# Part of a layer kernel rearranged: the state-space stage, its hand-over to the merge, one more expert block in the fixed schedule, and the latent stage

## The chip, the cores and the metric

The kernel runs on one core of a Trainium2 chip. The metric is the device time of one execution in microseconds, and the median of several runs is compared. Every time below is from one execution of the kernel before that was recorded with the hardware profiler, unless it says otherwise. TensorE is PE (its weight load PEld), VectorE DVE, ScalarE ACT, GpSimd POOL and SyncE SP.

## The reference, cut to what matters

Two transformer-like blocks run over 512 tokens of 1024 channels, in fp32. The parts that the change touches:

- State-space mixer: a projection gives x, B, C (24 tiles of 128 channels), a gate z (16 tiles) and a step width per head; a causal convolution of 4 taps and SiLU follow; then, in chunks, scores, states and outputs of 32 heads in 4 groups; at the end `y * silu(z)`, divided in each group by its root mean square (`rsqrt(mean(y*y) + 1e-6)`).
- Merge: `merged = g0 * y_att + g1 * y_pool + g2 * y_ssm`, with `g = sigmoid(h @ w_gate)`. The third gate is a product of h with 1024 columns, and `y_ssm` a product of the mixer's 2048 channels with `w_ssm_o`.
- Experts: each token goes to 2 of 16 experts, `(silu(x @ w1) * (x @ w3)) @ w2`, 512 wide.
- Latent projection of the second block: h @ w (448 columns), two root-mean-square norms of 256 and 128 channels, and a rotary embedding whose angles come from the positions.

## The kernel before

The program is a row of stages. In each, every engine has its own list of instructions and the lists are tied by semaphores; between two stages all engines meet. Matrix products at full precision are made of three: each fp32 operand is split into a high part (ACT writes it, rounded to the reduced fp32 type) and a low part (a subtraction on DVE), and PE multiplies high by high, high by low and low by high. So a weight tile has a chain: DMA, high part on ACT, low part on DVE, product on PE.

**State-space stage** (`ssm_stage`, from L1188). It forms 41 weight tiles of 1024x128, in the order of `ssm_tiles`: one for the step widths, 6 convolution tiles of group 0, and then for each group i the first four convolution tiles of group i+1, the four gate tiles of group i and the last two convolution tiles of group i+1. Tile t lies in `parts[t % 2]`, so its high part (`high`, L1415) waits for the product of tile t-2. `low` (L1543) is DVE's. The product is L1293, 24 matmuls of 128x512. PE's list for a group (from L1388) is: a tile, `turn_b` (L1307), a tile, `turn_x` 0 and 1 (L1315), a tile, `turn_x` 2 and 3, `chunk_products` (L1325), a tile, three `state`, `rows` and four times {a tile, `rows`, `heads`}, a tile, `squares`, a tile, `squares`. In the last group only the four gate tiles are left, and so the places before them are empty. `turn_x` waits until all six convolution tiles of its group have been convolved (L1558, L1560), bent (ACT's Tanh, L1443) and multiplied (L1576). `turn_b` waits for `std_done` of the group before, as both use bank 2. ACT's `root` (L1487) is a Sqrt, DVE's `invert` (L1686) a reciprocal, and then come four `normalise` passes (L1694). SP first stores x to DRAM and loads four small vectors (L1257 to L1263), and only then the next weight tiles; ACT waits for all four (L1493) before its other work on tile 0.

**Merge** (`merge_stage`, L1822). It works in halves, which are weight tiles of 1024x256 (`Halves`, L548: four slots of raw data, two of parts; `products` is L588, 48 matmuls each). For the third gate there are 12: 4 of the gate, 8 of `w_ssm_o` in two phases. DVE's `low(phase)` (L1914) makes the low parts of the mixer's output when a phase begins. Beside this DVE forms 8 strips of another product (`LaterStrips`, L1757): each is 2 MB from DRAM through a ring of two halves and 8 passes of DVE (`matvec`, L1787 and L1789). They are put behind the half-tiles of `STRIP_AT = (0, 1, 2, 4, 5, 6, 8, 9)`, and PE sums the first four (`ada.sums`) ahead of half-tile 6.

**Experts** (`experts_stage`, L2369). There is one block of 128 rows for each of the 16 experts, in a fixed, overlapped schedule. Rows beyond an expert's 128 go to further blocks, made in a loop of 7 with a condition (L2409, L2463, L2541, L2601): load, products in plain fp32 (L2469, L2482), nothing overlapped from one block to the next. In the recorded execution this loop's body ran once. The combine stage then gathers the rows (L2629).

**Latent** (`latent_stage`, L2675). SP loads the positions and the weights in the stage itself (L2697, L2698). PE's list is the angle product, four projections and two mean squares; ACT then takes a Sqrt of each, and DVE a reciprocal (L2750) and the scaling (L2753). The stage before it is `norm_stage` (L479).

## Time and profile before

| | |
|---|---|
| Median of 3 runs | 2955.51 us (2948.24 to 2959.59) |
| The profiled execution, its own time | 2950.82 us |
| Its span, first to last instruction | 2949.1 us |
| Mean granted TensorE clock | 0.922 of full speed |
| PE busy | 2589.5 us (88% of the span) |
| DVE busy | 1732.4 us (59%) |
| ACT busy | 1110.3 us (38%) |
| POOL busy | 47.6 us (2%) |

Busy time is an engine's sum over the whole span. What a part of the change can be worth is read from the stage it lies in: from the pieces of PE's time in which PE stood still there, and from what ended each of them. The state-space stage lies between 558 and 945 us, the merge from there to 1097 us, the experts' end and the combine stage around 1500 to 1600 us, and the latent stage between 1621 and 1676 us.

### The profile page before, as it was taken

Reading aid. Unit: us, or ns where it says so; the run is one execution under the profiler, and the core shown is the slowest. Engines: PE = TensorE matmul, PEld = TensorE weight load, DVE = VectorE, ACT = ScalarE, POOL = GpSimd, SP = SyncE. Lnnn points to the kernel's source line nnn. Section 1 sums busy time; section 2 is a strip of 40 time slices with the busy share of each in tenths; the row PEclk is TensorE's granted clock in tenths of the full one; section 3 lists DMA queues with packets and bytes.
Section 4 is the critical chain, followed back from the end, with each engine's and each line's share of the span. In section 5 each row is a group of like instructions: output and inputs, shape, how many; then the busy total and the mean of one; then the engine's idle time right before and its main releaser. Section 6 shows DMA issues by size and latency. Waiting matters only on the chain. (4 is left out here: it accounts for less than half of the span.)

```text
span 2949.1 us, 32640 instructions
## 1 busy us (share of the span) xinstructions
PE 2589.5 (88%) x12891; PEld 2014.7 (68%) x12891; DVE 1732.4 (59%) x2355; ACT 1110.3 (38%) x1586; POOL 47.6 (2%) x145
## 2 busy tenths in 40 slices
PE   7999799789987998499985698899997667799998
PEld 6777588567765875288862256788886666688886
DVE  6877625277776664599954364633447963643334
ACT  4333322135543222478842133532324123342333
POOL 0000000000000000100001000000000000000000
PEclk8999699899997999799997799999998788899999
DMA  7666537122212832499971121233231203223230
GB/s 252 222 213 205 196 96 271 44 72 64 65 51 71 287 128 87 163 392 417 414 281 64 53 66 57 72 100 88 98 100 17 31 2 114 86 86 100 87 100 29
DMA packets 285059, 393.61 MB, mean 133 GB/s; under 512 B 21400, under 2 KB 209291, under 8 KB 276204
## 3 DMA queue, kind: packets, MB, share of 16 engines
q1 hardware_dynamic: 277068, 361.65, 36.2%
q0 software_dynamic: 5392, 20.97, 1.8%
q10 hardware_dynamic: 2448, 8.91, 0.7%
q8 instruction: 102, 1.67, 0.2%
q14 instruction: 49, 0.40, 0.0%
HBM read 361.10 MB, written 30.41 MB: 133 GB/s over the span
## 5 line engine op out<-in xcount | busy, mean ns | idle before, releaser
L3248 PE MATMUL banks<-big,tail_w_parts 128*128 128x512 f32 x1920 | 444.0, 393 | 16.6 <-DVE tail_w_parts L3405 16.6
L3248 PEld LDWEIGHTS banks<-big,tail_w_parts 128*128 128x128 f32 x1920 | 363.9, 190 | 95.1 <-DVE tail_w_parts L3405 17.2
L3248 PE MATMUL banks<-h_parts_second,tail_w_parts 128*128 128x512 f32 x1440 | 332.9, 392 | 12.8 <-DVE h_parts_second L3430 12.8
L3405 DVE TENSOR_TENSOR tail_w_parts<-w_second,tail_w_parts 128x2048 fp32r<-128x2048 f32 x70 | 160.3, 2292 | 284.2 <-ACT tail_w_parts L3309 284.2
L3248 PEld LDWEIGHTS banks<-h_parts_second,tail_w_parts 128*128 128x128 f32 x1440 | 272.1, 189 | 71.0 <-issue 14.4
L1293 PE MATMUL banks<-h_parts,ssm_w_parts 128*128 128x512 f32 x984 | 244.0, 406 | 23.4 <-DVE ssm_xbc L1598 15.9
L1293 PEld LDWEIGHTS banks<-h_parts,ssm_w_parts 128*128 128x128 f32 x984 | 189.1, 195 | 71.7 <-DVE ssm_w_parts L1546 25.0
L2191 DVE TENSOR_TENSOR expert_parts<-w,expert_parts 128x2048 fp32r<-128x2048 f32 x96 | 219.4, 2289 | 30.7 <-ACT expert_parts L2187 30.3
L3309 ACT ACTIVATE tail_w_parts<-w_second 128x2048 fp32r<-128x2048 f32 x70 | 133.8, 1914 | 266.4 <-PE banks L3248 266.4
L2187 ACT ACTIVATE expert_parts<-w 128x2048 fp32r<-128x2048 f32 x96 | 183.4, 1916 | 60.2 <-PE banks L2198 60.2
L2198 PE MATMUL banks<-expert_parts,expert_xt 128*128 128x512 f32 x768 | 182.1, 397 | 5.1 <-DVE expert_xt L2563 5.1
L2198 PEld LDWEIGHTS banks<-expert_parts,expert_xt 128*128 128x128 f32 x768 | 145.6, 191 | 35.7 <-DVE expert_xt L2563 5.7
L597 PE MATMUL banks<-h_parts,ssm_parts 128*128 128x512 f32 x576 | 135.7, 398 | 14.7 <-DVE ssm_parts L586 11.5
L890 PE MATMUL banks<-h_parts,qkv_parts 128*128 128x512 f32 x552 | 145.5, 416 | 3.4 <-SPq L155 3.4
L597 PE MATMUL banks<-h_parts,front_parts 128*128 128x512 f32 x576 | 134.4, 395 | 8.5 <-DVE front_parts L586 6.4
L597 PEld LDWEIGHTS banks<-h_parts,ssm_parts 128*128 128x128 f32 x576 | 110.7, 193 | 39.8 <-DVE ssm_parts L586 12.5
L3439 DVE TENSOR_TENSOR tail_q<-tail_r 128x512 f32<-128x512 f32 x64 | 41.4, 688 | 159.7 <-ACT tail_r L3332 159.7
L597 PEld LDWEIGHTS banks<-h_parts,front_parts 128*128 128x128 f32 x576 | 109.6, 191 | 32.7 <-DVE front_parts L586 6.5
L890 PEld LDWEIGHTS banks<-h_parts,qkv_parts 128*128 128x128 f32 x552 | 106.1, 199 | 36.8 <-issue 11.4
L1095 DVE SCALAR_TENSOR_TENSOR attention_mod_sum<-w,silu_c,attention_mod_sum 128x512 f32<-128x512 f32 x168 | 126.1, 751 | 5.1
L3332 ACT ACTIVATE tail_r<-banks,cols 128x512 f32<-128x512 f32 x64 | 40.5, 685 | 204.9 <-PE banks L3248 204.9
L2198 PE MATMUL banks<-expert_parts,expert_ht 128*128 128x512 f32 x384 | 94.1, 402 | 4.5 <-DVE expert_ht L2568 4.5
(628 smaller groups left out, 3821.0 us busy)
## 6 DMA issues: line engine op xcount, KB each, us to landing
w_second<-in_mlp_w_dram SPq DMA_DIRECT2D x64, 1024.0 KB, 5.4
w<-in_w_in_dram SPq DMA_DIRECT2D x65, 512.0 KB, 4.0
w<-in_w_exp_gate_dram SPq DMA_DIRECT2D x32, 1024.0 KB, 7.7
w<-in_w_exp_up_dram SPq DMA_DIRECT2D x32, 1024.0 KB, 7.4
w<-in_w_exp_down_dram SPq DMA_DIRECT2D x32, 1024.0 KB, 8.8
w<-in_mod_mix_w_dram SPq DMA_DIRECT2D x24, 1024.0 KB, 5.0
w<-in_mod_ffn_w_dram SPq DMA_DIRECT2D x24, 1024.0 KB, 5.1
w<-in_w_in_dram SPq DMA_DIRECT2D x16, 1024.0 KB, 6.5
```

The lines of the kernel that those rows point to most:

```text
L597: mm = pe.matmul(out, self.parts[:, n % 2, w, kk, f * P:(f + 1) * P], x[:, v, kk, :], start=(start and kk == 0 and j == 0), stop=(stop and ...
L890: mm = pe.matmul(ps[:, bank, :], parts[:, j, w, kk, :], k.hp[:, x, kk, :], start=(kk == 0 and n == 0), stop=(kk == KD - 1 and n == 2))
L1095: ins = dve.scalar_tensor_tensor(out=acc, in0=w, scalar=by, in1=acc, op0=ALU.mult, op1=ALU.add)
L1293: mm = pe.matmul(ps[:, t % 2, :], parts[:, t % SPLITS, w, kk, :], k.hp[:, x, kk, :], start=(kk == 0 and j == 0), stop=(kk == KD - 1 and j ...
L2187: act.activation(self.high_part(h), self.raw(h), ACT.Copy).then_inc(self.high_done, 1)
L2191: dve.tensor_tensor(self.low_part(h), self.raw(h), self.high_part(h).bitcast(F32), ALU.subtract).then_inc(self.low_done, 1)
L2198: mm = pe.matmul(out, x[:, v, first + kk, :], self.tile(h, w, kk), start=(start and kk == 0 and j == 0), stop=(stop and kk == KE - 1 and j ...
L3248: mm = pe.matmul(ps[:, bank(n, f), :], w_part(n, w)[:, kk, f * P:(f + 1) * P], x[:, v, kk, :], start=(first_chunk(n) and kk == 0 and j == ...
L3309: act.activation(w_part(n, 0), raw_half(k, n), ACT.Copy).then_inc(s["high_done"], 1)
L3332: act.activation(r[:, c % 2, :], ps[:, bank(n, c % HT), :], ACT.Relu, bias=k.cols[:, b1 + at:b1 + at + 1]).then_inc(s["relu_done"], 1)
L3405: dve.tensor_tensor(w_part(n, 1), raw_half(k, n), w_part(n, 0).bitcast(F32), ALU.subtract).then_inc(s["low_done"], 1)
L3439: dve.tensor_tensor(q[:, c % 2, :], r[:, c % 2, :], r[:, c % 2, :], ALU.mult).then_inc(s["squared"], 1)
```

## The change

1. The store of x moves from the state-space stage to the first merge, behind its first loads; the four small vectors are loaded in the pool stage, ahead of the first state-space weight tiles there.
2. The low parts of tiles 7 to 40 are formed by GpSimd. Tiles 0 to 6 stay with DVE.
3. Sqrt and reciprocal of the group norm become `Ln` and `Exp(-0.5 ...)` on ACT, and `root` moves in ACT's list behind the next group's first tile. ACT and DVE finish a group's last convolution tile right behind that tile.
4. In the last group the gate tiles are placed further ahead, and PE multiplies the first two gate halves of the merge (4 output tiles) between `rows`, `heads` and `squares`. ACT and DVE form these halves and the third. The merge starts with its half-tile 2, and `STRIP_AT` becomes (1, 2, 3, 4, 5, 6, 8, 9).
5. The experts' fixed schedule has 17 blocks: the 17th is the first of the further blocks, its expert read from a register. The loop has 6 turns and no longer prepares the next block's rows.
6. The latent stage's loads are issued in the norm stage before it. PE starts with a projection, the angle product and the mean squares are put between projections, and the norms take `Ln` and `Exp` as well.

The diff, cut to its core ("..." marks what is left out; renamed buffers and loop bounds NE to NS are left out throughout):

```diff
@@ class Halves @@
+    def product(self, pe, n, f, x, out, final):
+        pe.wait_ge(self.low_done, n + 1)
+        for kk in range(KD):
+            for j, (w, v) in enumerate(((0, 0), (0, 1), (1, 0))):
+                mm = pe.matmul(out, self.parts[:, n % 2, w, kk, f * P:(f + 1) * P], x[:, v, kk, :], start=(kk == 0 and j == 0),
+                               stop=(kk == KD - 1 and j == 2))
+        if final:
+            mm.then_inc(self.half_used, 1)
@@ ssm_stage @@
     def more(i, n):
+        if i + 1 == G_SSM:
+            return {0: place["gate", i, 0], 2: place["gate", i, 1], 4: place["gate", i, 2], 5: place["gate", i, 3]}.get(n)
...
+        sums_bank = lambda i: 2 if i + 1 < G_SSM else 4
...
         def _(sp):
             k.clear(sp)
-            sp.dma_start(k.x_store, k.x[:].rearrange("p k t -> p (k t)")).then_inc(s["x_stored"], 16)
-            ...
             sp.wait_ge(s["w_low"], TILES)
-            for n in range(2):
-                halves.load(sp, halves.first["merge_ssm"] + n)
+            halves.load(sp, base)
+            halves.load(sp, base + 1)
+            sp.wait_ge(s["y_done"], KG * G_SSM)
+            halves.load(sp, base + 2)
+            halves.load(sp, base + 3)
...
         def _(pool):
+            for t in range(FIRST, TILES):
+                pool.wait_ge(s["w_high"], t + 1)
+                pool.wait_ge(s["w_low"], t)
+                pool.tensor_tensor(parts[:, t % SPLITS, 1], raw[:, t % RAWS], parts[:, t % SPLITS, 0].bitcast(F32),
+                                   ALU.subtract).then_inc(s["w_low"], 1)
...
         def _(pe):
-            for i in range(G_SSM):
+            for i in range(G_SSM - 1):
...
+            i = G_SSM - 1
+            tile_at(i, 0)
+            turn_b(i)
+            turn_x(i, 0)
+            turn_x(i, 1)
+            tile_at(i, 2)
+            turn_x(i, 2)
+            turn_x(i, 3)
+            chunk_products(i)
+            state(i, 0)
+            state(i, 1)
+            state(i, 2)
+            rows(i, 0)
+            for f in range(2):
+                tile_at(i, 4 + f)
+                rows(i, f + 1)
+                heads(i, f)
+            pe.wait_ge(s["z_gated"], KG * G_SSM - 1)
+            halves.product(pe, base, 1, k.hp, ps[:, 1, :], final=False)
+            rows(i, 3)
+            heads(i, 2)
+            pe.wait_ge(s["z_gated"], KG * G_SSM)
+            halves.product(pe, base, 0, k.hp, ps[:, 0, :], final=True)
+            heads(i, 3)
+            halves.product(pe, base + 1, 1, k.hp, ps[:, 3, :], final=False)
+            squares(i, range(KG))
+            halves.product(pe, base + 1, 0, k.hp, ps[:, 2, :], final=True)
...
             def root(i):
                 act.wait_ge(s["ms_done"], KG * (i + 1))
-                act.activation(std, ps[:, 2, :], ACT.Sqrt, ...).then_inc(s["std_done"], 1)
+                act.activation(std, ps[:, sums_bank(i), :], ACT.Ln, scale=1.0 / (KG * P), bias=k.eps_rms[:]).then_inc(s["std_done"], 1)
+                act.wait_ge(s["std_done"], i + 1)
+                act.activation(rstd, std, ACT.Exp, scale=-0.5).then_inc(s["norm_step"], 1)
...
-            act.wait_ge(s["small_loaded"], 64)
+            act.wait_ge(k.small_loaded, 64)
...
                 tile_at(i, 0)
+                follow(place["conv", i, NC - 1] + 1, last=True)
+                if i:
+                    root(i - 1)
                 copy_b(i)
...
+                    if i + 1 == G_SSM and f == 0:
+                        ...
+                        halves.high(act, base)
+                    if i + 1 == G_SSM and f == 2:
+                        act.wait_ge(s["tile_done"], TILES)
+                        halves.high(act, base + 1)
...
-                root(i)
+            root(G_SSM - 1)
+            halves.high(act, base + 2)
...
         def _(dve):
             def low(t):
-                if t < TILES:
+                if t < FIRST:
...
                 tile_at(i, 0)
+                follow(place["conv", i, NC - 1] + 1, last=True)
                 if i == 0:
                     ends()
-                else:
-                    invert(i - 1)
...
+                    if i + 1 == G_SSM and f in (0, 3):
+                        halves.low(dve, base + f // 3)
...
-            invert(G_SSM - 1)
             normalise(G_SSM - 1, range(KG))
+            halves.low(dve, base + 2)
@@ merge_stage @@
-    STRIP_AT = (0, 1, 2, 4, 5, 6, 8, 9)
+    STRIP_AT = (1, 2, 3, 4, 5, 6, 8, 9)
+    done = 2 if last else 0
...
             if last:
-                halves.load(sp, base + 2)
-                halves.load(sp, base + 3)
                 load_strip(0)
             halves.load(sp, base + 4)
             halves.load(sp, base + 5)
             if last:
                 sp.dma_start(k.x[:].rearrange("p k t -> p (k t)"), k.x_store).then_inc(s["x_back"], 16)
+            else:
+                sp.dma_start(k.x_store, k.x[:].rearrange("p k t -> p (k t)")).then_inc(k.x_stored, 16)
...
-            for n in range(N):
+            for n in range(done, N):
@@ pool_stage, SP @@
+            for half in range(2):
+                sp.dma_start(k.d_col[half * P_SSM:(half + 1) * P_SSM, :], ...).then_inc(k.small_loaded, 16)
+            for dst, name in ((k.dt_bias, "dt_bias"), (k.a_log, "a_log")):
+                sp.dma_start(dst[:], ...).then_inc(k.small_loaded, 16)
             for t in range(4):
                 sp.wait_ge(halves.low_done, base + PER + t // 2 + 1)
                 load_ssm(k, sp, t)
@@ experts @@
+NS = NE + 1
...
-            step(dve.tensor_copy(plan_f[:, SPILL:], end[0:1, NE - 1:NE]))
+            step(dve.tensor_scalar(plan_f[:, SPILL:], end[0:1, NE - 1:NE], -1.0, 0.0, ALU.add, ALU.max))
...
+            further = sp.value_load(m.plan[0:1, 0:1], min_val=0, max_val=NE - 1)
-            for n in range(NE):
-                if n + 2 < NE:
+            for n in range(NS):
+                if n + 2 < NS:
                     for h in range(4):
-                        m.load(sp, n + 2, h)
+                        m.load(sp, n + 2, h, further if n + 2 == NE else None)
...
-            with pe.Fori(0, SPILL) as n, pe.If(n < blocks):
+            with pe.Fori(0, SPILL - 1) as n, pe.If(n < blocks):
+                turn_spilled(n)
...
@@ latent_stage @@
+class LatentLoads:
+    def __call__(self, sp):
+        sp.dma_start(self.pos[:], self.k.ins["positions_2"]).then_inc(self.done, 16)
+        sp.dma_start(self.w, self.k.ins["mla_w_in_2"][0].rearrange("(k p) n -> p k n", p=P)).then_inc(self.done, 16)
...
+            pe.wait_ge(loads.done, 32)
+            project(0)
+            pe.wait_ge(s["freq_ready"], ROPE)
+            pe.wait_ge(s["pos_ready"], 1)
+            pe.matmul(ps[0:ROPE, 0, :], freq[:], pos[:], start=True, stop=True).then_inc(s["angle_done"], 1)
+            project(1)
+            project(3)
+            mean_square(0)
+            project(2)
+            mean_square(1)
...
-                step(dve.reciprocal(std[:, j, :], std[:, j, :]))
```

## Rows read from the trace of the kernel before

**Rows 1.** The page, section 5: busy, mean ns of one, idle before.

```profile
L2191 DVE TENSOR_TENSOR expert_parts<-w,expert_parts 128x2048 fp32r<-128x2048 f32 x96 | 219.4, 2289 | 30.7 <-ACT expert_parts L2187 30.3
```

**Rows 2.** What PE waited for between 560 and 945 us: total, times, longest.

```profile
PE banks L1293 <- DVE ssm_xbc L1598: 15.9, 1, 15.9
PE banks L1322 <- DVE ssm_xbc L1576: 14.4, 4, 6.3
...
PE banks L1329 <- DVE w L1645: 6.6, 3, 2.2
PE banks L1312 <- ACT ssm_sq L1489: 2.4, 1, 2.4
...
PE banks L1378 <- ACT ssm_sq L1485: 2.1, 1, 2.1
```

**Rows 3.** Busy time in 700 to 784 us: PE, PEld, DVE, ACT, POOL, clock, DMA.

```profile
700.00:784.00 84.00, 78.48 (x412) 59.95 (x411) 64.19 (x86) 40.31 (x82) 0.00 (x0) 0.98 0.24 63
```

**Rows 4.** Groups of instructions in 700 to 784 us, by line.

```profile
L1546 DVE TENSOR_TENSOR ssm_w_parts<-w,ssm_w_parts 128x1024 fp32r<-128x1024 f32 x10 | 12.2, 1224 | 5.6 <-ACT ssm_w_parts L1420 5.5
L1420 ACT ACTIVATE ssm_w_parts<-w 128x1024 fp32r<-128x1024 f32 x10 | 10.6, 1055 | 25.8 <-PE banks L1293 25.8
...
L1688 DVE RECIPROCAL ssm_sq<-ssm_sq 128x512 f32<-128x512 f32 x1 | 3.3, 3346 | 0.0
...
L1489 ACT ACT_TABLE_LOAD x1 | 1.3, 1283 | 0.0
...
L1489 ACT ACTIVATE ssm_sq<-banks,eps_rms 128x512 f32<-128x512 f32 x1 | 0.7, 688 | 0.0
```

**Rows 5.** Timeline around 590 us: start, length, instruction, idle before.

```profile
585.61 0.20 ACT L1494 ACTIVATE ssm_a_log<-ssm_a_log 32x1 f32<-32x1 f32 x1 [24.31 <-DMA ssm_a_log<-in_a_log_dram]
...
590.16 23.55 PE L1293 MATMUL banks<-h_parts,ssm_w_parts 128*128 128x512 f32 x96 [15.88 <-DVE ssm_xbc L1598]
```

**Rows 6.** GpSimd's own instructions, by line and shape.

```profile
L3242 POOL TENSOR_SCALAR vec<-cols 128x8 f32<-128x8 f32 x1 | 2.3, 2332 | 0.1
...
L1140 POOL TENSOR_TENSOR mod<-mod,cols 128x48 f32<-128x48 f32 x2 | 0.5, 285 | 354.2 <-ACTq L146 354.2
...
L3229 POOL TENSOR_TENSOR vec<-cols,mod 128x8 f32<-128x8 f32 x2 | 0.4, 204 | 326.7 <-POOLq L146 326.7
```

**Rows 7.** Timeline, PE at the end of the last group and after.

```profile
887.70 3.08 PE L1322 MATMUL banks<-ident,ssm_xbc 128*128 128x128 f32 x12 [6.32 <-DVE ssm_xbc L1576]
...
950.07 46.25 PE L597 MATMUL banks<-h_parts,ssm_parts 128*128 128x512 f32 x192 [11.53 <-DVE ssm_parts L586]
```

**Rows 8.** The merge: one window, DMA issues of 945 to 1000 us, one strip's passes.

```profile
960.00:970.00 10.00, 10.00 (x46) 8.29 (x45) 4.19 (x4) 4.29 (x4) 0.00 (x0) 1.00 1.08 416
...
merge_ssm_ada_ring<-in_w_ada_dram SPq DMA_DIRECT2D x8, 1024.0 KB, 5.7
...
979.40 5.48 DVE L1789 SCALAR_TENSOR_TENSOR merge_ssm_ada_acc<-merge_ssm_ada_ring,silu_c,merge_ssm_ada_acc 128x512 f32<-128x512 f32 x7
```

**Rows 9.** Timeline of the experts: two starts, two stores, the gather.

```profile
1380.57 11.16 PE L2198 MATMUL banks<-expert_parts,expert_xt 128*128 128x512 f32 x48
...
1398.26 2.09 PE L2198 MATMUL banks<-expert_parts,expert_xt 128*128 128x512 f32 x8
...
1535.30 0.34 ACTq L2506 DMA_DIRECT2D expert_rows<-experts_y  x1
...
1567.08 0.36 ACTq L2553 DMA_DIRECT2D expert_rows<-experts_y  x1
1573.57 0.99 POOL L2629 DMA_INDIRECT expert_parts_plain<-expert_rows,slots  x1 [348.87 <-POOLq L146]
```

**Rows 10.** Timeline of the latent stage.

```profile
1629.70 0.42 DVE L2738 CAST latent_pos<-latent_pos_i 1x512 f32<-1x512 int32 x1 [8.30 <-DMA w_second<-in_mla_w_in_dram]
...
1632.13 30.74 PE L2714 MATMUL banks<-h_parts_second_plain,w_second 128*128 128x512 f32 x64
...
1674.91 0.75 DVE L2753 SCALAR_TENSOR_TENSOR ckv<-banks,cols,latent_std 128x512 f32<-128x512 f32 x1
```

280 lines of the change are left out of this document (148 added, 132 removed).

## The prediction

> **What bounds the kernel now.** I read first the windows of the state-space stage: in one full group PE works 78.5 of 84.0 us and DVE 64.2 [rows 3]. PE sets the pace, so a part of the change is worth what it takes out of PE's standing still. The view of waits names those pieces [rows 2]: 15.9 us once, 14.4 us in four waits for the last convolved tile, 6.6 us in three waits of `chunk_products`, 2.4 us and 2.1 us around the last group. The timeline adds 11.5 us between the state-space stage and the merge's first product [rows 7]. Outside that stage I read the timeline of the experts' end [rows 9], where a last block runs alone, and of the latent stage [rows 10], which waits for its own load and ends in a chain of single operations.
>
> **Part 1, small vectors ahead.** PE stands 15.88 us before its third tile [rows 5]. ACT had idled 24.31 us for the last of the small vectors, and its high part of that tile is queued behind that wait. Now they are loaded in the pool stage, ahead of the four weight tiles with which this stage starts, and tile 2 follows tile 1. The DVE work behind it starts as early, so all of it is gain: **-15.9**. The moved DMAs cost SP about as long as now, before weight loads that are not needed until the stage starts; I take 0. The store of x, 2 MB among the first merge's loads, also 0: it waits for nothing and PE is served from halves loaded before. Together they could cost 0 to 2.
>
> **Part 2, low parts on GpSimd.** No row has this operation at 1024 columns. The two-input passes that it has take 204 ns at 8 columns and 285 at 48 [rows 6], so 2.0 ns a column and an estimate of 2.3 us at 1024, against DVE's 1.22 [rows 4]. From below, DVE's own 1.22; from above I take the odd 2.33 us of an 8-column pass [rows 6] as a fixed cost on top, 4.4. The chain from the end of tile t to tile t+2 is 1.06 (high part, rows 4) + 2.3 + some 0.6 of semaphores = 4.0 us, and PE has the tile between them, 24 x 46.25/192 = 5.8 us [rows 7], to cover it. So the longer pass is hidden, and DVE loses 34 passes. Cost 0. What the relief gives is the three waits of `chunk_products`: the low part stood on DVE ahead of `weigh`; about 0.4 of each 2.2 us stays: **-5.4** [rows 2].
>
> The trace has no GpSimd pass beside DVE's, so it shows nothing on whether they hinder each other; I put +2 into the sum for it and keep 0 and 40 as ends (40: half of 34 x 2.3 us lands on PE's path). The Trainium skill, SBUF — State Buffer, section Who interferes with whom, speaks against this part: a DVE instruction with two SBUF inputs and a GpSimd instruction that reads SBUF lock each other out for a whole instruction. No run here shows it yet; by it the convolution and score passes would each wait up to one GpSimd pass, which is the second rival below.
>
> **Part 3, the group's end.** The last tile of a group is now bent and multiplied at once, so the four waits of `turn_x` go: 14.4, of which 6.3 belong to the last group (part 4), so **-8.1**. But a wait comes that isn't there today. `turn_b` needs `std_done` of the group before, and ACT now reaches `root` only after the high part of tile t+2, which waits for the tile that PE has just done. So PE stands for 1.06 + a Tanh of 0.7 (a 128x512 pass, as the Sqrt) + the table load 1.28 + Ln 0.7 [rows 4] + 0.3 = 4.0 us, in groups 1 and 2: **+8.0**. The reciprocal of 3.35 us goes from DVE [rows 4], which is off PE's path there.
>
> **Part 4, last group and hand-over.** PE's work from the last convolution tile to the merge's third half-tile is the same before and after, in another order. Of the standing, 2.4 + 6.3 + 2.1 + 11.5 = 22.3 goes [rows 2, 7]. What comes: 4.0 at `turn_b` (part 3), and the stage's end. After the last `squares` PE has one product of 5.8; beside it run Ln and Exp 1.4, four 128x512 passes of 0.7, the third half's low part 2.3 [rows 1] and some 0.7 between them, 7.2 in all, and 0.5 to meet: PE stands 1.9. PE also ran slow after its gaps (12 short matmuls took 3.08 us, rows 7); I take -4 for that, from 0 to -7. Sum: -22.3 + 4.0 + 1.9 - 4 = **-20.4**.
>
> **The merge's queue.** PE comes to the merge 20 us earlier in its work, the DMA queue does not. In units of 1 MB SP issues: strip 0 (2 units), two halves, x (2), two halves, then strip 1 (2). At 416 GB/s a unit takes 2.5 us [rows 8]; the tenth lands at 25.2 + some 3 (a unit's landing is 5.7, so 3.2 over its transfer) = 28.4 after the stage begins. Strip 1's second four passes take 3 of its 6 us, so DVE is free at 31.4. Its next work is `low(1)`, which could begin after two half-tiles and ACT's first high part, 0.5 + 23.1 + 0.7 = 24.3. **+7** (0 to +10). Today there are four half-tiles before `low(1)`, which cover it.
>
> **Part 5, the 17th expert block.** A block of the fixed schedule takes 1398.26 - 1380.57 = 17.69 us. Today the last store of the schedule is issued at 1535.30 and that of the loop's block at 1567.08, 31.78 later [rows 9]. Now it comes 17.69 later and all behind it (landing, six empty turns, the gather at 1573.57) as now: **-14.1**. The block reads 6 MB more behind the same DMA queue as its 16 forerunners, at the same pace.
>
> **Part 6, latent stage.** It begins at 1621.4 (1629.70 - 8.30, rows 10) and ends at 1675.7, 54.3 us. Now, at 30.74/64 = 0.48 a pass of PE [rows 10]: projections 30.7, the angle product 1.0 and the first mean square 1.9 between them, then a square 0.8, one mean square 1.2, Ln and Exp 1.5, one scaling 0.8: 37.9, and 0.4 to start. **-16.0**. Bounds: 14, if PE starts at its low clock for longer, and 17.5.
>
> **Sum.** -15.9 - 5.4 + 2 - 8.1 + 8.0 - 20.4 + 7 - 14.1 - 16.0 = -62.9. From the profiled execution's 2950.8 us that is 2887.9; the median of the runs lies 4.7 higher, so **2892**. Differences under about 0.5% (15 us) can't be told from no change.
>
> **Rivals.**
> - *The queue keeps up* (strip 1 lands in time, PE's clock falls less often): the +7 is gone and the slow matmuls too, 2892 - 7 - 4 = 2881. For it: the merge's queue stood at 416 GB/s only while it had a backlog [rows 8]. Against it: there are 10 units in the order given whatever the pace.
> - *DVE and GpSimd hinder each other.* 34 passes of 2.3 us are 78 us in which DVE may stand; it gives up 34 x 1.22 = 42. A full group then has 64.2 - 12.2 - 3.3 + 23 = 72 of 84 us for DVE, still less than PE, but in bunches at the group's change and before `heads`. A quarter of 78 on PE's path gives 2912. For it: DVE is at 64 of 84 already [rows 3]. By the Trainium skill's rule named above this should be seen in full.
> - *GpSimd is too slow, slower than before.* Where tiles follow each other directly, the chain has 5.8 us: it decides from a pass of 5.8 - 1.7 = 4.1 us on. Each microsecond more costs up to 34. At 7 us a pass (the fixed 2.33 and twice the estimate) it is 34 x 2.9 = 99 and the time 2991; to be slower than before takes 6 us. Against it: the slope of two rows. The Trainium skill, GPSIMD Engine Reference, section 3.1, gives 4497 ns for a two-input fp32 pass of 2048 columns; by it a pass here is some 2.2 us, on the forecast's side.
> - *Part 5 or 6 gives half*: 2892 + 15 = 2907, within the range. The block's count is data: had the loop's body not run, part 5 would cost 17.7. It did run once.
>
> **How the numbers follow.** Forecast 0.5; queue keeps up 0.2; hindering 0.2; half of part 5 or 6 0.06; slow GpSimd 0.04. The range takes in the first three with the bounds of the unknown costs: below 2881 the larger ends of parts 4 and 6, about 2874; above 2912 a little more, 2914. Faster by over 0.5%: all but the last and the worst of the hindering, 0.94; within 0.5% 0.02; slower 0.04.
>
> **What would show it.** PE's third tile right behind the second. POOL busy by some 34 x 2.3 = 78 us more, in passes of 2.3, beginning about 1.1 us after each tile's end. No wait of PE for L1576's successor, but a new one of about 4 us before `turn_b` in three groups, ended by ACT's Ln. The third half-tile's product under 3 us behind the stage's last. In the merge, PE waiting some 7 us for the first low part of the mixer's output. Two stores of the experts 17.7 us apart and no matmul of the loop. The latent stage 38 us long. DVE's convolution passes would be longer, or further apart, if the engines hinder each other. The forecast is wrong if PE waits for weight parts in mid-group, or if any of the six parts shows its wait moved rather than gone.

## The result, and the profile after

The changed kernel takes **2916.2 us** in the median of 4 runs (2906.1 to 2918.1), beside 2954.4 for the kernel before on the same chip: ratio 0.9865, 95% interval 0.9835 to 0.9894, so 1.1 to 1.7% faster. The profiled execution took 2915.5 us with a span of 2913.7, where the one before had 2949.1: 35.4 us less, against the 62.9 of the prediction's sum. The time lies 24 us above the forecast of 2892, 2 us above the upper end of the range (2914) and 4 us above the 2912 of the second rival.

First the page of the kernel after: its span, and busy time and share of each engine.

```profile
span 2913.7 us, 32687 instructions
## 1 busy us (share of the span) xinstructions
PE 2583.0 (89%) x12907; PEld 2020.6 (69%) x12907; DVE 1738.2 (60%) x2320; ACT 1124.6 (39%) x1598; POOL 130.8 (4%) x180
```

Then one line's instructions, GpSimd's low parts (duration min/median/max). They take 2.4 us, where the prediction estimated 2.3, and begin some 1.2 us after a tile's end.

```profile
L1302 POOL TENSOR_TENSOR ssm_parts<-w,ssm_parts x34: 2337/2400/2922, 603.6 to 894.2; 128x1024 fp32r<-128x1024 f32 x34
```

The timeline of PE, kernel after, from the state-space stage to the residual stage: start, length, instruction, and the idle time before it. It answers to [rows 2, 5, 7]. Of the waits over 2 us one is left out, 2.63 us at 603.50, which stands in both kernels.

```profile
561.45 12.55 PE L1319 MATMUL banks<-h_parts,ssm_parts 128*128 128x512 f32 x48 [4.35 <-DVE ssm_parts L1613]
577.21 23.66 PE L1319 MATMUL banks<-h_parts,ssm_parts 128*128 128x512 f32 x96 [3.21 <-DVE ssm_xbc L1665]
...
616.14 0.76 PE L1326 MATMUL banks<-ssm_parts_plain,ones 32*128 32x128 f32 x2 [6.91 <-DVE ssm_parts_plain L1692]
645.37 2.08 PE L1355 MATMUL banks<-ssm_parts_plain 128*128 128x128 f32 x8 [6.14 <-DVE w L1712]
715.02 1.08 PE L1338 MATMUL banks<-ident,ssm_xbc 128*128 128x128 f32 x4 [3.82 <-ACT ssm_sq L1542]
798.78 0.63 PE L1338 MATMUL banks<-ident,ssm_parts_plain 128*128 128x128 f32 x4 [3.82 <-ACT ssm_sq L1542]
882.83 1.09 PE L1338 MATMUL banks<-ident,ssm_xbc 128*128 128x128 f32 x4 [3.82 <-ACT ssm_sq L1542]
949.60 23.65 PE L615 MATMUL banks<-h_parts,ssm_parts 128*128 128x512 f32 x96 [2.58 <-PEq L148]
985.74 24.55 PE L615 MATMUL banks<-h_parts,ssm_parts 128*128 128x512 f32 x96 [12.50 <-DVE h_parts L1983]
1088.89 16.48 PE L615 MATMUL banks<-ys,ssm_parts 128*128 128x512 f32 x62 [2.71 <-DVE ys L2173]
```

The reader should see three things. The old waits of 6.32 and 11.53 us are gone, and of the 15.88 us before the third tile 3.21 are left, with another cause [rows 2, 5, 7]. The forecast wait of `turn_b` is there, 3.82 us in each of three groups, ended by ACT's Ln (L1542). And three waits are longer than forecast or new: 6.91 us before the front's end (2.3 in the kernel before), 6.14 before the `chunk_products` of group 0 (2.19 before), and 12.50 in the merge.

Where the 35.4 us come from, stretch by stretch, both profiled executions (the state-space stage from PE's first tile to the merge's third half-tile, which is 950.07 + 46.25/2 = 973.2 before [rows 7]; the merge from there to the residual stage's first product, at 1098.90 before and 1088.89 after):

| stretch | before | after | change | forecast |
|---|---|---|---|---|
| state-space stage | 412.7 | 388.2 | -24.6 | -39.8 |
| merge | 125.7 | 139.3 | +13.6 | +7 |
| residual, norm, routing | 132.2 | 134.3 | +2.1 | 0 |
| experts, to the gather | 342.5 | 332.2 | -10.3 | -14.1 |
| combine to the end of the latent stage | | | -16.7 | -16.0 |
| ahead of the state-space stage, and behind the latent stage | | | +0.5 | 0 |

### The profile page after: what moved, and what is told of

Same layout as the page of the kernel before. It is cut to its first block and busy times, and to the rows that moved or that the text cites. A ratio compares the mean times of both kernels' runs of the same rounds, so it can differ in the third digit from the quotient of the medians.

```text
span 2913.7 us, 32687 instructions
## 1 busy us (share of the span) xinstructions
PE 2583.0 (89%) x12907; PEld 2020.6 (69%) x12907; DVE 1738.2 (60%) x2320; ACT 1124.6 (39%) x1598; POOL 130.8 (4%) x180
## 5 line engine op out<-in xcount | busy, mean ns | idle before, releaser
L3351 PEld LDWEIGHTS banks<-big,tail_w_parts 128*128 128x128 f32 x1920 | 363.0, 189 | 94.8 <-DVE tail_w_parts L3508 17.2
L3351 PE MATMUL banks<-h_parts_second,tail_w_parts 128*128 128x512 f32 x1440 | 332.4, 391 | 12.8 <-DVE h_parts_second L3533 12.8
L1319 PE MATMUL banks<-h_parts,ssm_parts 128*128 128x512 f32 x984 | 245.1, 407 | 10.7 <-DVE ssm_parts L1613 7.0
L2265 DVE TENSOR_TENSOR expert_parts<-w,expert_parts 128x2048 fp32r<-128x2048 f32 x102 | 233.2, 2290 | 34.5 <-ACT expert_parts L2261 33.4
L1319 PEld LDWEIGHTS banks<-h_parts,ssm_parts 128*128 128x128 f32 x984 | 189.7, 196 | 59.5 <-DVE ssm_parts L1613 11.8
L2261 ACT ACTIVATE expert_parts<-w 128x2048 fp32r<-128x2048 f32 x102 | 194.9, 1916 | 65.7 <-PE banks L2272 65.6
L2272 PE MATMUL banks<-expert_parts,expert_xt 128*128 128x512 f32 x816 | 195.5, 400 | 5.1 <-DVE expert_xt L2635 5.1
L2272 PEld LDWEIGHTS banks<-expert_parts,expert_xt 128*128 128x128 f32 x816 | 155.9, 193 | 38.5 <-DVE expert_xt L2635 5.7
L615 PE MATMUL banks<-h_parts,ssm_parts 128*128 128x512 f32 x480 | 115.7, 404 | 16.7 <-DVE h_parts L1983 14.1
L615 PEld LDWEIGHTS banks<-h_parts,ssm_parts 128*128 128x128 f32 x480 | 93.9, 196 | 38.1 <-issue 14.9
L2272 PE MATMUL banks<-expert_parts,expert_ht 128*128 128x512 f32 x408 | 100.0, 401 | 4.5 <-DVE expert_ht L2640 4.5
```

The source lines that it names most:

```text
L615: mm = pe.matmul(out, self.parts[:, n % 2, w, kk, f * P:(f + 1) * P], x[:, v, kk, :], start=(start and kk == 0 and j == 0), stop=(stop and ...
L1319: mm = pe.matmul(ps[:, t % 2, :], parts[:, t % SPLITS, w, kk, :], k.hp[:, x, kk, :], start=(kk == 0 and j == 0), stop=(kk == KD - 1 and j ...
L2261: act.activation(self.high_part(h), self.raw(h), ACT.Copy).then_inc(self.high_done, 1)
L2265: dve.tensor_tensor(self.low_part(h), self.raw(h), self.high_part(h).bitcast(F32), ALU.subtract).then_inc(self.low_done, 1)
L2272: mm = pe.matmul(out, x[:, v, first + kk, :], self.tile(h, w, kk), start=(start and kk == 0 and j == 0), stop=(stop and kk == KE - 1 and j ...
L3351: mm = pe.matmul(ps[:, bank(n, f), :], w_part(n, w)[:, kk, f * P:(f + 1) * P], x[:, v, kk, :], start=(first_chunk(n) and kk == 0 and j == ...
```

## The experiments

The run times scatter by about 5 us around their medians, so differences of 3 us between two kernels are read from their traces: each table row below gives the two stretches of the table above for one profiled execution. The runs come from several chips, on which the kernel before had medians from 2948.6 to 2954.4 us, so kernels from different chips are compared by the ratio. Four traces in which the state-space stage is the same code (the changed kernel, strip_late, x_late, x_s1) give 387.3 to 391.3 us for it. A difference of under 4 us in that column says nothing by itself; there the single waits are compared.

| kernel | time, us | ratio to before, 95% interval | state-space | merge |
|---|---|---|---|---|
| changed kernel | 2916.2 | 0.9865 (0.9835 to 0.9894) | 388.2 | 139.3 |
| low_dve | 2913.0 | 0.9869 (0.9831 to 0.9907) | 387.4 | 139.2 |
| low_late_pool | 2906.4 | 0.9852 (0.9812 to 0.9892) | 383.8 | 138.5 |
| root_first | 2915.7 | 0.9879 (0.9839 to 0.9919) | 390.3 | 140.3 |
| root_now | 2910.7 | 0.9855 (0.9828 to 0.9882) | 384.0 | 139.2 |
| strip_late | 2912.8 | 0.9868 (0.9830 to 0.9905) | 391.3 | 140.4 |
| x_late | 2905.9 | 0.9842 (0.9818 to 0.9867) | 390.8 | 133.4 |
| x_s1 | 2899.8 | 0.9826 (0.9805 to 0.9848) | 387.3 | 126.5 |
| old_order | 2908.3 | 0.9846 (0.9823 to 0.9870) | 384.1 | 139.3 |
| old_x_s1 | 2897.4 | 0.9814 (0.9795 to 0.9834) | 384.1 | 127.3 |
| old_x_s1_split | 2891.5 | 0.9793 (0.9771 to 0.9814) | 381.2 | 128.7 |
| recip_x_s1 | 2884.6 | 0.9787 (0.9764 to 0.9810) | 373.7 | 126.1 |
| recip_x_s1_split | 2881.3 | 0.9770 (0.9751 to 0.9789) | 366.3 | 126.3 |
| recip_x_s1_split_raw | 2877.4 | 0.9756 (0.9736 to 0.9776) | 364.1 | 127.3 |
| before_pool | 2941.5 | 0.9971 (0.9957 to 0.9985) | 403.9 | 126.5 |
| before_block17 | 2939.9 | 0.9969 (0.9955 to 0.9984) | | |

**1. low_dve**, the low parts back on VectorE.

```diff
-            for t in range(FIRST, TILES):
-                pool.wait_ge(s["w_high"], t + 1)
...
-                if t < FIRST:
+                if t < TILES:
                     dve.wait_ge(s["w_high"], t + 1)
```

> The changed kernel with all 41 low parts of the state-space stage's weight tiles on VectorE again, GpSimd without any; all else as changed. In the changed kernel PE waits 6.9 us before turn_small (2.3 in the kernel before) and 6.1 us before group 0's chunk_products (2.2 before), and the VectorE passes next to them lie beside GpSimd passes and take 2.5 to 3.8 us where they took 0.7 to 2.3. Theory (GpSimd's passes hold VectorE's up): both waits go back to 2.3 and some 2.2 us, the VectorE passes to 0.7 and 2.3 us, and with the slower clock after the gaps some 10 to 13 us come back; the later chunk_products waits grow from 1.5 to some 2.2 us each. Time 2904 to 2907. Rival (VectorE is only later in its queue, from the new order of tanh and silu): the long waits stay, VectorE has 41 passes of 1.2 us more, time 2916 to 2922.

Measured 2913.0. PE's wait at the front's end fell from 6.91 to 3.93 us and that of group 0 from 6.14 to 2.30, and from the stage's begin to group 1's `turn_b` it gained 7.1 us (146.5 in place of 153.6). By these waits and by VectorE's passes the theory of hindrance holds; its time, 2904 to 2907, was missed, because what came back there was lost again in the later groups. To the merge it is 387.4 against 388.2, and the ratio is the same, so part 2 bought next to nothing in the changed kernel. In the later groups the waits differ by only 0.35 us a group; the rest of the loss is PE's clock, as the tile behind the wait of 3.82 us took 8.1 us in low_dve and 6.8 and 7.3 in the changed kernel, at mean granted clocks of 0.96 and 0.95 for the two groups in place of 0.98 and 0.97. No run here tells why the clock differed, so a part of the balance can be chance. Why VectorE was not relieved shows in the view of groups by shape: name and shapes, count, busy us, mean ns. First a full group of VectorE's passes of the changed kernel (705 to 789 us):

```profile
L1751 DVE SCALAR_TENSOR_TENSOR ys_plain<-ys_plain,ssm_xbc 128x512 f32<-128x512 f32 x4 | 6.5, 1624 | 0.1
L1717 DVE TENSOR_TENSOR w<-w,ssm_parts_plain 128x512 f32<-128x512 f32 x3 | 5.0, 1669 | 0.1
L1749 DVE SCALAR_TENSOR_TENSOR ssm_xbc<-ssm_xbc,d_col,banks 128x512 f32<-128x512 f32 x4 | 3.0, 741 | 0.0
L1732 DVE TENSOR_TENSOR w<-w,ssm_decay 128x512 f32<-128x512 f32 x2 | 2.8, 1420 | 0.1
L1712 DVE TENSOR_TENSOR w<-banks,ssm_small 128x512 f32<-128x512 f32 x4 | 2.7, 685 | 2.3 <-PE banks L1348 2.3
L1625 DVE TENSOR_SCALAR ssm_xbc<-ssm_u,ssm_parts_plain 128x512 f32<-128x512 f32 x1 | 2.3, 2339 | 0.2 <-ACT ssm_u L1481 0.2
```

Then the same group of low_dve (697 to 782 us), whose line numbers are five lower:

```profile
L1608 DVE TENSOR_TENSOR ssm_parts<-w,ssm_parts 128x1024 fp32r<-128x1024 f32 x10 | 12.2, 1224 | 7.9 <-ACT ssm_parts L1468 7.7
L1744 DVE SCALAR_TENSOR_TENSOR ssm_xbc<-ssm_xbc,d_col,banks 128x512 f32<-128x512 f32 x4 | 3.0, 741 | 0.0
L1746 DVE SCALAR_TENSOR_TENSOR ys_plain<-ys_plain,ssm_xbc 128x512 f32<-128x512 f32 x4 | 2.8, 691 | 0.1
L1707 DVE TENSOR_TENSOR w<-banks,ssm_small 128x512 f32<-128x512 f32 x4 | 2.7, 684 | 0.0
L1712 DVE TENSOR_TENSOR w<-w,ssm_parts_plain 128x512 f32<-128x512 f32 x3 | 2.1, 692 | 0.1
L1727 DVE TENSOR_TENSOR w<-w,ssm_decay 128x512 f32<-128x512 f32 x2 | 1.4, 694 | 0.1
L1620 DVE TENSOR_SCALAR ssm_xbc<-ssm_u,ssm_parts_plain 128x512 f32<-128x512 f32 x1 | 0.5, 543 | 0.0
```

Ten passes of 1.22 us, 12.2 in all, leave VectorE; its other passes grow by 14.5 us in the group (L1751 3.7, L1717 2.9, the convolution's L1627 2.2, and so on). Passes with `banks`, a PSUM tensor (PSUM holds the products' results here, SBUF all else), among their inputs don't grow (741 ns in both, 685 and 684). The ones that do have both inputs in SBUF and lie beside a GpSimd pass, and one is a tensor_scalar with a single input; each grows by at most about a GpSimd pass. The Trainium skill, SBUF — State Buffer, section Who interferes with whom, says just this: two SBUF inputs contend with a GpSimd instruction that reads SBUF, and so does VectorE in a two-port mode, which tensor_scalar can enter. The trace agrees in every one of these rows.

**2. low_late_pool**, tiles 7 to 11 on VectorE, the rest on GpSimd (`FIRST + 5` in place of `FIRST` in both places).

> The changed kernel with the low parts of weight tiles 7 to 11 (front and the first half of group 0) on VectorE and those from tile 12 on GpSimd. Theory of hindrance: the loss is where VectorE is dense, in the front and in group 0's first half, and it is gone here (10 to 13 us), while the later groups stay as in the changed kernel: time 2903 to 2906, 1 us under the kernel with all of them on VectorE. Rival (GpSimd hinders everywhere, a bit per group): half of it, 2910, and the kernel with all on VectorE is clearly ahead. Second rival (not GpSimd at all): 2916 to 2918.

Measured 2906.4, and 383.8 us for the stage: 4.4 less than the changed kernel. To group 1's `turn_b` it gained the same 7.1 us as low_dve, but kept only part of it, because the two groups after it took 85.2 us each where the changed kernel has 83.8 and 84.1: the waits are the same, and the granted clock is 0.96 in both, with the tile behind the wait at 8.1 and 8.2 us. The place is as expected; the size is under half of the 10 to 13 us, by the trace as by the ratio (0.9852 for 0.9865).

**3. root_first and root_now**, part 3's new wait. root_first puts `root(i - 1)` and the last tile's Tanh ahead of the tile's high part; root_now puts the root ahead of that Tanh too:

```diff
+                if i:
+                    follow(place["conv", i, NC - 1] + 1)
+                    root(i - 1)
+                    follow(place["conv", i, NC - 1] + 1, last=True)
                 tile_at(i, 0)
                 follow(place["conv", i, NC - 1] + 1, last=True)
-                if i:
-                    root(i - 1)
                 copy_b(i)
```

> The changed kernel with ACT's root of the group before (Ln, Exp) ahead of the high part of the tile after next, in place of behind it. Theory: PE's wait of 3.82 us before turn_b, in groups 1, 2 and 3, comes from that order alone; with the root first its Ln is done while PE is still in the tile (5.8 us, root some 4.0 from its start), so the three waits fall under 0.5 us, and the tile after each (6.8 to 7.3 us now) goes back to 5.8: -11.5 and up to -3, time 2901 to 2906. Rival: the tile after next is then late, because its high part stands behind the root, and a wait of 2 to 4 us comes at that tile instead: 2914 to 2918.

> The changed kernel with ACT's root of the group before (Ln, Exp) ahead of the last convolved tile's Tanh, where the run root_first had it behind that Tanh. In root_first the root began only at 708.66, because the Tanh had waited 4.26 us for a convolution whose first pass lay beside a GpSimd pass and took 2.35 us for 0.55; PE still waited 2.85 us three times. Theory (the wait is a matter of what stands ahead of the root on ACT): the root now runs in that gap, the three waits before turn_b are gone, and turn_x, which needs the Tanh behind it, waits 0 to 1 us: -8 to -11 in the state-space stage against the changed kernel. Rival (the last tile's chain, convolution, Tanh and silu, is late whatever the order, and turn_x or weigh takes the wait over): -2 or less. In either case a part of it comes to the front of the merge, which the DMA queue holds: whole time 2905 to 2912 by the theory, 2914 to 2917 by the rival.

root_first missed its theory: 2915.7, a time in the rival's range but not for the rival's reason, as the three waits were still 2.85 us. The root now stood behind a Tanh that waited 4.26 us for a convolution, whose first pass had met a GpSimd pass. In root_now the waits at `turn_b` are gone, and `chunk_products` waits 4.50 us where it waited 1.54; 2910.7 and 384.0 us for the stage, 4 us gained of the 11.5 that had stood in the waits, which lies between the theory (8 to 11) and its rival (2 or less). So the order on ACT was the cause of the wait, but behind it the last tile's chain over VectorE was nearly as late.

**4. strip_late, x_late and x_s1**, the merge's queue. strip_late is `STRIP_AT = (1, 3, 4, 5, 6, 7, 8, 9)`; x_late issues the load of x behind the merge's last load; x_s1 also issues strip 1 ahead of half-tiles 6 and 7:

```diff
...
             if last:
-                sp.dma_start(k.x[:].rearrange("p k t -> p (k t)"), k.x_store).then_inc(s["x_back"], 16)
...
+                load_strip(1)
             for n in range(N):
                 if n + 6 < N + 4:
                     halves.load(sp, base + n + 6)
-                if last and n in STRIP_AT[:-1]:
+                if last and n in STRIP_AT[1:-1]:
                     load_strip(STRIP_AT.index(n) + 1)
             if last:
+                sp.dma_start(k.x[:].rearrange("p k t -> p (k t)"), k.x_store).then_inc(s["x_back"], 16)
                 sp.wait_ge(s["x_back"], 16)
```

> The changed kernel with the second and later strips of the merge's vector one place later in VectorE's and the DMA queue's order (1, 3, 4, 5, 6, 7, 8, 9), so that the first low parts of the mixer's output no longer stand behind strip 1. Theory: PE's 12.5 us before the second phase of the merge are VectorE standing 11.2 us for strip 1; without it the low parts begin after the second half-tile's low part and PE waits 0 to 2 us: -10 to -12, time 2904 to 2906, if the later strips find their place. Rival: VectorE and the DMA queue only move the wait, and PE stands 5 to 10 us later in the merge, for a half-tile or for the sums: 2912 to 2918.

> The changed kernel with the 2 MB load of x, needed by nothing in the merge, moved from ahead of half-tiles 6 and 7 and strip 1 to behind the merge's last load. Theory (the 12.5 us wait at the merge's second phase is the one DMA queue's backlog, 10 units of 1 MB ahead of strip 1's end): strip 1 lands 2 x 2.5 = 5 us sooner, PE waits 7 to 8 us, and the merge ends 4 to 5 us sooner: 2911 to 2912. Rival (the ring of two half-strips, load, use, load, sets the pace and not the bytes ahead of it): the wait stays over 11 us and the time 2915 to 2917. Against both: if the load of x is late at the merge's end, its landing shows as a wait of 5 us there.

> x_late, and strip 1 also ahead of half-tiles 6 and 7 in the DMA queue. In x_late strip 1 landed 24.0 us after the merge's begin (29.3 in the changed kernel), VectorE idled 6.4 us for it and PE waited 7.2 us. Theory (the queue's order is the whole cause): its first half can be issued once VectorE has used strip 0's, some 11 us after the begin, and lands at about 18; VectorE is done with it when the first low part is due, and PE waits 0 to 2 us: 5 us less than x_late, 2900 to 2902. Rival (half-tiles 6 and 7, now later, are missed next, or VectorE lacks the time for four strips before the sums): PE waits 3 to 6 us at a later half-tile or at the sums, 2905 to 2908.

VectorE's timeline in the changed kernel: it stands 11.22 us for strip 1, and the low parts of the mixer's output (L1983), for which PE waits, begin only behind it, 35.3 us after the third half-tile.

```profile
978.87 0.49 DVE L1852 TENSOR_SCALAR merge_ssm_ada_acc<-merge_ssm_ada_ring,silu_c 128x512 f32<-128x512 f32 x1 [11.22 <-DMA merge_ssm_ada_ring<-in_w_ada_dram]
979.40 5.47 DVE L1854 SCALAR_TENSOR_TENSOR merge_ssm_ada_acc<-merge_ssm_ada_ring,silu_c,merge_ssm_ada_acc 128x512 f32<-128x512 f32 x7
984.91 4.91 DVE L1983 TENSOR_TENSOR h_parts<-ys_plain,h_parts 128x512 fp32r<-128x512 f32 x8
```

strip_late took that wait away, and PE stood 10.46 us at the sums instead, which need strip 3 (its timeline):

```profile
974.44 22.01 PE L615 MATMUL banks<-h_parts,ssm_parts 128*128 128x512 f32 x96 [1.54 <-DVE h_parts L1983]
1006.91 6.96 PE L1867 MATMUL banks<-ones,merge_ssm_ada_acc 128*128 128x1 f32 x32 [10.46 <-DVE merge_ssm_ada_acc L1854]
```

The merge stayed at 140.4 us: the rival. x_late had strip 1 land 5.3 us sooner, PE's wait 7.20, the merge 133.4. x_s1 took the rest: the same line as in the changed kernel's timeline, and then 126.5 us for the merge, as before the change (125.7).

```profile
945.79 23.64 PE L615 MATMUL banks<-h_parts,ssm_parts 128*128 128x512 f32 x96 [2.58 <-PEq L148]
971.55 22.02 PE L615 MATMUL banks<-h_parts,ssm_parts 128*128 128x512 f32 x96 [2.12 <-DVE h_parts L1984]
```

So the cause is the order of the one queue's loads, shown by undoing it: 2 MB of x and two half-tiles, none of them needed yet, stood ahead of the strip that was. That the strips' place alone didn't help says that the strips must come sooner, not be used later.

**5. before_pool**, part 2 alone in the kernel before.

> The kernel before with part 2 alone: the low parts of weight tiles 7 to 40 on GpSimd, nothing else changed. Theory (GpSimd's passes stretch VectorE's neighbours): PE's waits in the front and before group 0's chunk_products grow by some 4 us each, and the full groups gain 1 to 2 us each; on the whole 0 to +8: 2951 to 2960. Forecast of the prediction for this part: -5.4 + 2, 2948. The second rival of the prediction (a quarter of the passes' 78 us on PE's path): 2965 to 2975.

Measured 2941.5, ratio 0.9957 to 0.9985: a **gain** of 8.2 us (2949.7 for the kernel before on that chip), outside what any theory named, and the state-space stage 403.9 against 412.7. The wait at the front's end did grow, from 2.32 to 5.28 us. But a full group went from 84.0 to 79.3 us (`turn_x` at 723.22 and 802.54), with one wait of 1.57. The changed kernel, with the same GpSimd passes and part 3 on top, takes 83.8. That opened the question of the next two runs.

**6. old_order**, part 3 undone in groups 0 to 2 (`follow(..., last=True)` on ACT and VectorE in the last group alone, `root(i)` at the end of its own group), and **old_x_s1**, **old_x_s1_split**, the same with x_s1 and with tiles 7 to 11 on VectorE.

> The changed kernel with part 3 undone in groups 0 to 2: ACT's last Tanh and VectorE's last silu of a group stand where they stood before, and the root (still Ln and Exp) at the end of its own group. The last group and the merge as changed. In the kernel before with GpSimd's low parts alone (run before_pool) a full group took 79.3 us from turn_x to turn_x and had one wait of 1.57 us, in the changed kernel it takes 83.8 us with waits of 3.82 and 1.55 us. Theory (part 2 alone had already taken those waits away, and part 3 only adds turn_b's wait and brings the one of chunk_products back): groups 1 and 2 fall to 79.5 us each and the wait at turn_b goes, -10 to -13 in the state-space stage: 2903 to 2906. Rival (the wait at turn_b, 3.82 us, is all that part 3 costs, and the old waits of 3.15 us at turn_x come back): 81 to 83 us a group, 2911 to 2915.

> old_order and x_s1 together. If the state-space stage's gain and the merge's are independent, their sum: 11.5 + 14 = some 25 us below the changed kernel, 2891 (2888 to 2896). Rival (what the state-space stage gains is waited for in the merge, since the merge's first load is issued when the stage begins): the gain cannot be lost there, as the merge's loads move along with its begin; the sum would be missed only by 3 to 5 us of slower clock.

> old_x_s1 with the low parts of weight tiles 7 to 11 on VectorE, those from 12 on on GpSimd. The changed kernel gained 9.8 us by this step (7.1 of it in the front and group 0 by the traces). Theory (the hindrance in front and group 0 is independent of the order at a group's end): another 5 to 8 us, 2884 (2882 to 2888). Rival (with the old order group 0 is not held up, as before_pool had no wait at group 0's chunk_products): only the wait before turn_small shrinks, -3: 2888 to 2890.

old_order missed its theory: 2908.3, and 83.3 us a group, not 79.5; the wait moved from `turn_b` back to `turn_x` and was 4.53 us. old_x_s1 (2897.4) has both gains, the stage's 4 and the merge's 12 us, so they are independent, but lies 6 us above its expectation, since the stage's gain was overrated. The further step gave 5.9 us (2891.5), in the 5 to 8 that it was to give, though above the 2882 to 2888 that were built on the missed 2891; the traces show 2.9 us of it in the stage (the front's wait 3.94 for 6.92) and none in the merge. The two timelines of the group's change tell old_order and before_pool apart. VectorE and GpSimd in old_order:

```profile
703.58 4.35 DVE L1626 SCALAR_TENSOR_TENSOR ssm_xbc<-ssm_u,ssm_parts_plain,ssm_xbc 128x512 f32<-128x512 f32 x3
...
711.27 2.83 DVE L1642 SCALAR_TENSOR_TENSOR ssm_xbc<-w,ssm_xbc 128x512 f32<-128x512 f32 x1
```

```profile
704.96 2.42 POOL L1302 TENSOR_TENSOR ssm_parts<-w,ssm_parts 128x1024 fp32r<-128x1024 f32 x1 [3.84 <-ACT ssm_parts L1473]
710.86 2.69 POOL L1302 TENSOR_TENSOR ssm_parts<-w,ssm_parts 128x1024 fp32r<-128x1024 f32 x1 [3.48 <-ACT ssm_parts L1473]
```

Both GpSimd passes meet VectorE passes with two SBUF inputs, on the chain that PE waits for: three convolution passes take 4.35 us for 2.33, one silu pass 2.83 for 0.68. In before_pool the first of the two meets the reciprocal of 3.35 us.

**7. recip_x_s1**, old_x_s1 with that reciprocal back, and two more steps on it.

```diff
             def root(i):
                 act.wait_ge(s["ms_done"], KG * (i + 1))
+                if i + 1 < G_SSM:
+                    act.activation(std, ps[:, sums_bank(i), :], ACT.Sqrt, scale=1.0 / (KG * P), bias=k.eps_rms[:]).then_inc(s["std_done"], 1)
+                    return
...
                 if i == 0:
                     ends()
+                else:
+                    invert(i - 1)
```

> old_x_s1 with the root of groups 0 to 2 as in the kernel before: a Sqrt on ACT and the reciprocal of 3.35 us on VectorE. old_order had 83.3 us from turn_x to turn_x and a wait of 4.53 us there, before_pool 79.3 and 1.57. By the two timelines the same three GpSimd passes lie at the group's change; in old_order two of them meet a convolution pass and a silu with two SBUF inputs (4.35 us for three passes in place of 2.33, 2.83 for 0.68), in before_pool the first meets the reciprocal, which has one input and is not stretched. Theory (what a GpSimd pass costs is settled by what VectorE happens to run beside it): the reciprocal, though 3.35 us more work for VectorE, takes the wait at turn_x to some 1.6 us and the group to 79.5: -3 to -4 a group, three times, 2886 to 2889. Rival (the reciprocal is 3.35 us more in front of the convolution, and before_pool was quicker for another reason): the wait grows to 6 us or more, 2899 to 2907.

> recip_x_s1 with the low parts of weight tiles 7 to 11 on VectorE, those from 12 on on GpSimd. old_x_s1 gained 5.9 us by this step. Theory (the front's wait of 6.9 us goes back to 3.9; group 0's first half is held up in either order): -3 to -6, 2881 to 2885. Rival (it moves the meetings of passes at the first group's change for the worse): no gain, 2887 to 2890.

> recip_x_s1_split with VectorE's two short passes on the first tile (the bias of the raw times, which free the first tile's PSUM bank) ahead of the low part of tile 3 in place of behind it. In the changed kernel PE's third tile waited 3.21 us for them. Theory (they wait only for tile 0, the low part for tile 1, so this order is all of that wait): the wait is gone, -3: 2878 to 2882. Rival (tile 2 then waits for tile 3's low part or the next eviction, or the later chain of the front, which is VectorE's, ends as late as before): 0 to -1.

VectorE in recip_x_s1, then GpSimd:

```profile
708.58 0.68 DVE L1645 SCALAR_TENSOR_TENSOR ssm_xbc<-w,ssm_xbc 128x512 f32<-128x512 f32 x1
709.18 3.35 DVE L1757 RECIPROCAL ssm_sq<-ssm_sq 128x512 f32<-128x512 f32 x1
712.44 0.45 DVE L1627 TENSOR_SCALAR ssm_parts_plain<-ssm_parts_plain 128x512 f32<-128x512 f32 x1
712.92 2.33 DVE L1629 SCALAR_TENSOR_TENSOR ssm_parts_plain<-ssm_parts_plain 128x512 f32<-128x512 f32 x3
```

```profile
709.67 2.41 POOL L1302 TENSOR_TENSOR ssm_parts<-w,ssm_parts 128x1024 fp32r<-128x1024 f32 x1 [3.86 <-ACT ssm_parts L1473]
```

The GpSimd pass lies wholly beside the reciprocal, which takes its 3.35 us as ever [rows 4], and the convolution behind it runs at 2.33. PE's timeline has the group at 79.3 us, as in before_pool, and the wait at 1.56:

```profile
715.90 1.09 PE L1348 MATMUL banks<-ident,ssm_xbc 128*128 128x128 f32 x8 [1.56 <-DVE ssm_xbc L1645]
795.24 1.09 PE L1348 MATMUL banks<-ident,ssm_parts_plain 128*128 128x128 f32 x8 [1.56 <-DVE ssm_parts_plain L1645]
```

The stage became 10.4 us shorter (384.1 to 373.7), and the ratio fell from 0.9814 to 0.9787, some 8 us. The theory's time was 2886 to 2889, and 2884.6 was measured. Its reason isn't shown, though, because the edit changed two things: it put 3.35 us of reciprocal on VectorE, and it took Exp and its table load off ACT ahead of ACT's next piece of work (the load that Tanh needs after a Sqrt comes only behind that piece). ACT's timeline tells what the second one did. First old_order, where this group's end has PE's tile at 697.66:

```profile
700.55 1.28 ACT L1544 ACT_TABLE_LOAD   x1
701.84 0.63 ACT L1544 ACTIVATE ssm_sq<-ssm_sq 128x512 f32<-128x512 f32 x1
702.38 0.58 ACT L1481 ACTIVATE ssm_u<-banks 128x512 f32<-128x512 f32 x1
```

Then recip_x_s1, where the same tile starts at 702.37, with the convolution that follows on VectorE:

```profile
704.55 0.69 ACT L1543 ACTIVATE ssm_sq<-banks,eps_rms 128x512 f32<-128x512 f32 x1
705.13 0.59 ACT L1481 ACTIVATE ssm_u<-banks 128x512 f32<-128x512 f32 x1
706.34 2.33 DVE L1629 SCALAR_TENSOR_TENSOR ssm_xbc<-ssm_u,ssm_parts_plain,ssm_xbc 128x512 f32<-128x512 f32 x3
```

Counted from the tile's start, a GpSimd pass begins at 7.30 us in both. In old_order ACT copies `ssm_u` at 4.72 us, and the convolution runs from 5.92 to 10.27, into that pass. In recip_x_s1 the copy comes at 2.76 and the convolution runs from 3.97 to 6.30, ahead of the pass. So, by the timelines, the first meeting went away because ACT was done 1.96 us sooner, and not because of the reciprocal, which VectorE reaches only behind it. The second meeting, that of the silu, is avoided because the last tile's convolution starts 0.72 us sooner: the silu begins at 12.79 in place of 13.61 us, and the next GpSimd pass at 13.20 in both. That convolution could have started as soon without the reciprocal: its input was ready at about 710.6, and the GpSimd pass ended at 712.08. This last step is an estimate from the rows of recip_x_s1; a run with Sqrt on ACT and no reciprocal on VectorE, which would settle it, wasn't made.

The front and group 0 on VectorE gave another 7.4 in the stage, of which the run time shows 3: 2.7 of the 7.4 are the 96 products of the front, the same code in both, which took 22.04 us at a granted clock of 1.00 and 24.73 at 0.89. The two passes of the raw times ahead of tile 3's low part took the third tile's wait of 3.21 us away altogether, with 2.2 us less for the stage: **2877.4 us**, 2.4% under the kernel before (interval 2.2 to 2.6%) and some 32 us under the changed kernel by the two ratios.

**8. before_block17**, part 5 alone.

> The kernel before with part 5 alone: the experts' fixed schedule of 17 blocks. In the changed kernel the stretch from the experts' first transposes to the gather shrank by 10.25 us where 14.1 were expected: 2.0 of the difference lie before the first store, 0.6 in the 16 periods, 1.5 behind the last store. Theory A (the start was slower because TensorE came to it at a lower clock, which the changed kernel's earlier stages cause, 0.69 against 0.78 granted in the first 17 us): here the start takes 45.6 us to the first store, as in the kernel before, and the stretch shrinks by 12 to 12.5. Theory B (the code of the new schedule itself, a register load ahead of SP's first issues, costs it): 47.6 us again, shrinking by 10.3. Time 2939 to 2942 by A, 2941 to 2944 by B; the prediction's term gives 2937 to 2940.

Measured 2939.9. From the first transposes (1234.45) to the gather (1564.07) it is 329.6 us, 12.8 less than before, and the first store came 45.7 us after the begin, as in the kernel before (45.6), not after 47.6 as in the changed kernel: theory A. The changed kernel came to the experts with PE granted 0.69 of full speed in the first 17 us where it was 0.78 in the kernel before; its first 48 products took 13.91 us, beside 12.60 before. Why it had the lower clock there was not tried.

## Why the prediction was right and wrong

**Part 1** stated -15.9, "tile 2 follows tile 1" and "all of it is gain". The wait for the small vectors is gone, but 3.21 us of a new one came, for VectorE's passes on tile 0 (L1665), which stand behind the low part of tile 3 and so behind tile 1. The third tile came 15.76 us after the stage's begin in place of 29.70: -13.9, of which 12.7 are the wait; the other 1.3 are the first 48 products, 12.55 us for 13.83, which no other trace repeats (13.65 to 14.05 in the rest). The run with the two passes moved shows that this order was the wait. It is a wait moved rather than gone, which the prediction names as a sign of being wrong.

**Part 2, the step that failed.** "Cost 0", with "-5.4" for `chunk_products` and "+2" for hindering. The pass itself was right, 2.4 us for 2.3, and it was hidden from PE. (The Trainium skill, GPSIMD Engine Reference, section 3.1, pointed to 2.2; the trace has 2.34 at least.) But the relief was counted as 34 passes taken from VectorE, with a flat 2 us against it, and VectorE got no relief at all: 12.2 us less and 14.5 us more in a full group. The front's last stretch (tile 2 to `turn_small`) became 3.1 us longer, and the next to group 0's `chunk_products` 3.7 us longer where it should have lost 1.8 and `turn_x`'s 1.7. Together that is 3.1 + 3.7 + 3.5 = 10.3 us. The terms of the stage without the +2 missed by 17.2: these 10.3, 2.0 of part 1, 3.7 in groups 1 and 2, and 1.2 of part 4; the +2 leaves the 15.2 of the table. low_dve shows GpSimd as the cause of 6.3 of the 10.3 (61.9 us from the third tile to group 0's `chunk_products`, for 68.2). It also shows how far the stage is from being a sum: without part 2 it took 387.4 us, where the forecast's other terms give 376.3. Measured on top of the other parts, part 2 cost 0.8 us (388.2 for 387.4) where -3.4 was forecast. The other 11 us are missing in low_dve as well: 3.2 to the third tile, 4.3 from group 2's `chunk_products` on, and the rest between; PE's clock has a share in them. `chunk_products` still waits 1.5 us in groups 1 and 2, for a forecast of 0.4. Nor was the rule of the second rival seen "in full", on PE's path: a quarter of 78 us would be 19.5. What counts is not how much, but which VectorE pass meets GpSimd's, and whether PE waits for that chain. With the same passes before_pool gained 8.2 us, more than the -3.4 of the forecast.

**Part 3** stated -8.1 + 8.0. The new wait was forecast 4.0 us and measured 3.82, ended by ACT's Ln, for the reason given; `turn_x` no longer waits. The step held in size. What it couldn't see is that part 2 changes the ground: with GpSimd's passes the kernel before had 1.57 us left at `turn_x`. Part 3 also put Exp and a second table load on ACT ahead of the next copy from PSUM, and took the reciprocal from VectorE. Undoing both together, on top of the old order, was worth some 8 to 10 us (recip_x_s1); the timelines put that down to ACT, and the reciprocal seems to have been off PE's path, as the prediction called it.

**Part 4** stated -20.4. From group 2's `chunk_products` to the third half-tile it is 134.3 us in place of 153.6, so -19.2. PE stood 2.58 us at the hand-over for a forecast of 1.9. That it came so near is in part luck: Ln and Exp each loaded a table (L1542 and L1544, 1.28 us each), where the sum had none, but the first load began 0.6 us before PE's last product, and the gaps that the sum had put between the passes weren't there.

**The merge's queue** stated +7, within 0 to 10, and the stretch became 13.6 us longer. Mechanism and place were right, the ten units, strip 1, the low parts behind it. Two terms were too small: VectorE does all eight passes of strip 1 (6.0 us) behind its first half's landing, 29.3 us after the stage's begin, where the sum had 3 us behind a landing at 28.4, so that the low parts begin at 35.3 in place of 31.4; and PE came back slow from the wait, 24.55 us for the 96 products that took 22.03 before, for which the sum had nothing here.

**Part 5** stated -14.1, measured -10.3. Alone in the kernel before it is -12.8, and the step that was too small there is "all behind it ... as now": from the last store to the gather it is 8.0 us in both kernels with 17 blocks, and was 6.5. Why is open. The other 2.5 us are the slower start (2.0) and the periods, 17.74 us each for 17.69. **Part 6** stated -16.0; to the first product behind the latent stage it is -16.7 (with the combine and the norm): right, with the projections starting at once and a mean square between them, as this timeline shows (the 10.30 us before the first product are the end of the stage before).

```profile
1603.03 10.01 PE L2795 MATMUL banks<-h_parts_second_plain,w_second 128*128 128x512 f32 x16 [10.30 <-PEq L148]
1612.97 1.07 PE L2809 MATMUL banks<-latent_pos,latent_freq 1*64 1x512 f32 x2
1613.96 14.14 PE L2795 MATMUL banks<-h_parts_second_plain,w_second 128*128 128x512 f32 x32
1628.04 1.98 PE L2802 MATMUL banks<-latent_sq,ones 128*128 128x512 f32 x4
```

The sum of the misses: 15.2 + 6.6 + 2.1 + 3.8 + 0.5 - 0.7 = 27.5 us, which is what lies between 62.9 and 35.4. The 2.1 are products behind the same waits, in the residual, norm and routing stretch, at a mean granted clock of 0.91 for 0.93. Most stalls that the forecast named went or came as said. It was wrong mainly by what came behind them: VectorE's passes beside GpSimd's, and strip 1 behind the loads ahead of it.

## What to carry to other kernels

Work given to GpSimd relieves VectorE only where VectorE meanwhile is idle or runs passes that don't grow beside it, as here those that read PSUM and the reciprocal; where both are released by the same event, as here by a tile's end, they meet each time, so look at the timeline of both engines pass by pass and not at the sum of busy time. A third engine can decide whether they meet: 1.96 us of ACT ahead of a copy moved a convolution into a GpSimd pass. When a stage comes sooner, list its DMA queue in order of issue and move whatever is not needed first behind what is: two lines gave 13 us here. And when several edits aim at the same wait, price them one on top of the other: part 2 alone was worth 8 us in the kernel before and nothing on top of the other parts. And when an edit that undoes two things helps, look in the trace for the one that did it before naming it.

## What the hardware showed unexpectedly

A VectorE pass with two SBUF inputs that meets a GpSimd pass doesn't slow down in proportion to its own length, it grows by up to nearly a whole GpSimd pass: 0.69 to 2.55 us (L1751), a 32x512 one 0.68 to 2.77, scans of 32x128 0.41 to 0.92 in the mean of four. GpSimd loses little in turn (2.34 to 2.92 us, median 2.40). And a Ln followed at once by an Exp loaded two tables of 1.28 us each, in all four groups.
